# Order of work around three token mixers: preparation of the third moved, taps and tails of the first moved, activation tables fetched earlier

## The chip, the cores and the metric

The kernel runs on one core of one Trainium2 chip. The metric is the device time of one execution, in microseconds. A core has five engines, each with its own instruction stream: TensorE (PE, matrix products and transposes), VectorE (DVE), ScalarE (ACT, activation functions from tables that have to be loaded), GpSimd (POOL) and SyncE (SP, which here only issues DMAs). They wait for each other by semaphores. SBUF is the on-chip memory of 128 partitions, PSUM the one into which PE writes.

## The reference

One inference step of a decoder of two layers, for a prompt of 256 tokens and eight sampled sequences of 4 tokens. All of it is in float32. One layer, cut to what matters:

```python
h = rmsnorm(x, lp['norm_g'])
proj = h @ lp['w_in']
qkv_a, z_a, beta_raw, alpha_raw, f_b, z_b, qkv_c, z_c, gate_raw = jnp.split(proj, offs, axis=-1)
# first mixer: gated delta rule
u_a, dn_buf_new = causal_conv(qkv_a, dn_buf, lp['conv_a'])   # 4 taps; the last 3 rows are an output
q_a, k_a, v_a = jnp.split(jax.nn.silu(u_a), [...], axis=-1)  # q_a, k_a: l2norm by head
o_a, dn_s_new = gated_delta_chunked(q_a, k_a, v_a, g_a, beta, dn_s)   # chunks, triangular systems
o_a = rmsnorm(o_a, lp['onorm_a']) * jax.nn.silu(z_a)
# second mixer: RWKV-7
f_mix = f_b + (prev - f_b) * lp['mu_b']
w_raw = lp['w0_b'] + jnp.tanh(wl_b) @ lp['w2_b'];  a_b = sigmoid(lp['a0_b'] + al_b @ lp['a2_b'])
kk = l2norm(heads(k_b * lp['kk_b']))
y_b, rw_s_new = rwkv7_scan(r_h, logw, k_h, v_h, -kk, kk * a_h, rw_s)
o_b = (groupnorm(y_b) + bonus) * jax.nn.silu(z_b)
# third mixer: block-sparse attention over the paged cache and the new keys
q_c = rope_partial(rmsnorm(heads(q_c), lp['qn_c']), pos)     # the same for k_c
o_c = moba_attention(q_c, pos, k_all, v_all) * jax.nn.silu(z_c)
up = jnp.einsum('blnc,ncd->blnd', jnp.stack([o_a, o_b, o_c], axis=2), lp['w_branch'])
x = x + jnp.sum(sigmoid(gate_raw + lp['b_gate']) * up, axis=2) @ lp['w_out']
x = x + jax.nn.sigmoid(x @ lp['w_pg'] + lp['b_pg']) * (ple @ lp['w_ple'])
```

Outputs are x of both kinds of tokens, the new keys and values, and the new states and last rows of the first two mixers.

## The kernel before

All 288 tokens (256 of the prompt, 32 sampled) go through as the columns of one matrix that lies transposed, 128 channels on the partitions. A projection is 8 matmuls of 128×128 weights by 128×288 for each 128 output channels (`project`, L1092). The weights come through a ring of four SBUF stages; SyncE loads one (L858), 1 MB for two such tiles, when the stage's last projection is done. Three PSUM banks take the projections in turn.

The order of the work is one list of steps, the same for all engines; each engine runs through it and does its part of each step (a method of the step's name in the engine's block). `mixer_steps()` gives the 306 steps of a layer's mixers in order: names with `a_` belong to the first mixer, `b_` to the second, `c_` to the third. `fillers()` gives the projections, cut into "leads" of one K-tile each (one matmul), and their small followers (`z_silu`, `g_tanh`). `schedule()` puts them together: the hand-written list FILL has a number for each mixer step, and so many fillers stand ahead of that step. PE works them off while the other engines prepare the step's operands. The semaphore counts (`S.count`) follow from the list.

The steps that the change and the prediction touch, with their lines:

- First mixer: `a_conv(c)` is the causal convolution of a third of the channels (VectorE L2190 to L2192, part of it on POOL L2735), `a_silu` its activation, `a_sq` the squares. `a_l2(i)` sums them on PE (`sum4`, L1161) and takes the inverse root on ScalarE by Ln and Exp; `a_spread(i)` spreads it by PE (`spread4`, L1168). `a_convout` copies the last three rows ("tails", VectorE L2172), transposes them on PE, evicts them on ScalarE and stores them by POOL (L2713). `a_scale(t)` and `a_pairs(t)` build the chunk matrices, `tri`, `lev_y` and `lev` the inverses of the triangles (PE L1253, L1269, L1275). `a_u(u)` are corrections, u = 2 the sampled sequences' (L1305). `a_sout(0..3)` are their new states: VectorE L2374 masks, PE L1340 multiplies, VectorE L2378 adds, POOL scales the next start (L2770) and stores.
- Second mixer: `b_hist`, `b_shiftout` and `b_mix` prepare the token shift (VectorE L2398 to L2403; POOL clears two buffers, L2790). `b_lora(i)` are the small products behind tanh and sigmoid (PE L1364), `b_kk` and `b_spread` an l2norm, then chunk matrices, triangles and states as in the first mixer, in two groups. `b_fin`, `b_sout`, `b_sdec` end the states, `b_norm1` to `b_norm6` the group norm.
- Third mixer: `c_rms(i)` has 4 of the 8 tiles of queries and keys for each i. ScalarE squares them, PE sums (L1161), ScalarE takes the inverse root; SyncE copies the eight-row halves of each head crosswise (L958), VectorE makes the rotation in three instructions (L2611 to L2613). `c_rope(i)` spreads the roots (L1168) and multiplies (L2619). `c_fetch_k`, `c_fetch_v` fetch pages of the cache (L966). `c_nat` transposes keys and values (PE L1019, ScalarE) and stores them; POOL clears CQX (L2813) and copies the sampled queries into it. `c_keys(g,j)` transposes the past keys; scores, softmax and products follow.

ScalarE has two tables in use, one with Tanh and one with Ln; both have Exp. `logs()` (L1677) loads the second one ahead of an instruction if the other is in place; before Tanh the compiler's own load comes (shown at L1685).

Of the kernel before, what the change touches and what calls it, by code (L numbers as in the profile page):

```python
# [23 lines left out]
US = CONV_W - 1 + LS  # L24
# [77 lines left out]
for _name, _k in PROWS:  # L102
# [95 lines left out]
    "c_turned": {"c_rms": (1, None)},  # L198
# [14 lines left out]
    "c_sw0": {"c_rms": (96, lambda st: st[2] == 0)},  # L213
    "c_sw1": {"c_rms": (96, lambda st: st[2] == 1)},
# [16 lines left out]
    "projected": {"p_a": (1, None), "p_z": (1, None), "p_ba": (1, None), "p_f": (1, None), "p_c": (1, None), "p_g": (1, None), "p_up": (1, None), "p_y": (1, None), "p_pg": (1, None), "p_ple": (1, None)},  # L231
    "square_sums": {"norm": (1, None), "a_l2": (1, None), "b_kk": (1, None), "b_bonus": (1, None), "c_rms": (1, None),
                "a_spread": (1, None), "b_spread": (1, None), "c_rope": (1, None)},
    "squares": {"x_in": (2, None), "p_ple": (2, lambda st: st[1] + 1 < DEPTH), "a_sq": (1, None), "b_kk": (1, None), "c_rms": (1, None)},
# [27 lines left out]
    "c_qx": {"c_nat": (1, lambda st: st[2] == 0)},  # L262
# [3 lines left out]
PROJECTIONS = ("p_a", "p_z", "p_ba", "p_f", "p_c", "p_g", "p_up", "p_y", "p_pg", "p_ple")  # L266
# [33 lines left out]
def mixer_steps():  # L300
# [77 lines left out]
    for g in range(2):  # L378
# [34 lines left out]
        add("b_norm6", g, 1)  # L413
        add("b_s0", g, 0)
# [56 lines left out]
def fillers():  # L471
# [44 lines left out]
    for m in range(4, 8):  # L516
# [6 lines left out]
FILL = [0, 0, 32, 6, 0, 10, 17, 0, 19, 0, 4, 0, 6, 3, 6, 3, 18, 2, 14, 3, 0, 1, 14, 3, 0, 0, 0, 0, 0, 1, 1, 0, 0, 0,  # L523
# [90 lines left out]
def program(nc, A, O):  # L614
# [6 lines left out]
    with ctx:  # L621
# [33 lines left out]
        CT = TRI[:, 896:896 + NA * 27]  # L655
# [52 lines left out]
        BAR1, BN1, BVN1, BRB1, BKK1, BY1 = part(512), part(2, 2, 128), part(2, 128), part(4, 128), part(1024), part(2, 128)  # L708
# [130 lines left out]
        turned = [(h + to, h + of, n) for h in (0, 64) for to, of, n in ((0, 8, 8), (8, 0, 8), (16, 16, 48))]  # L839

# [4 lines left out]
        def _(sp):  # L845
# [107 lines left out]
            def c_rms(l, i):  # L953
                evicted(sp, "p_c", l, 4 * i + 3)
                sp.wait_ge(S.sem("b_done"), S.count("b_done"))
                sp.wait_ge(S.sem("b_snew"), S.count("b_snew"))
                for to, of, n in turned:
                    sp.dma_start(CSW[to:to + n, i, :, :], QC[of:of + n, 4 * i:4 * i + 4, :]).then_inc(S.sem(f"c_sw{i}"), 16)  # L958
# [20 lines left out]
            def c_fetch_v(l, s):  # L979
                if s >= 4:  # L980
# [10 lines left out]
            def y_out(l, m):  # L991
# [8 lines left out]
                if m == 7:  # L1000
                    for name in ("kv_stored", "states_stored", "tail_rows_stored", "y_stored"):
# [3 lines left out]
                      c_rms=c_rms, c_fetch_k=c_fetch_k, c_fetch_v=c_fetch_v, p_up=p_up, y_out=y_out)  # L1005
# [9 lines left out]
        def _(pe):  # L1015
# [646 lines left out]
        def _(act):  # L1662
# [48 lines left out]
            def norm(l):  # L1711
                act.wait_ge(S.sem("param_done"), S.count("param_done"))
# [106 lines left out]
            def a_l2(l, i):  # L1819
                act.wait_ge(S.sem("square_sums"), S.count("square_sums"))  # L1820
# [55 lines left out]
            def a_norm4(l, t):  # L1876
                w = wid(t)
# [12 lines left out]
            def b_lora(l, i):  # L1890
# [966 lines left out]
```

## Time and profile before

| | us |
|---|---|
| median of three runs | 1285.93 |
| the three runs | 1288.49, 1282.99, 1285.93 |
| the profiled execution | 1283.79 |
| its span | 1281.9 |
| PE busy | 1234.9 (96%) |
| VectorE busy | 599.8 (47%) |
| ScalarE busy | 355.2 (28%) |
| POOL busy | 134.7 (11%) |

The profile is of one execution. Its span runs from the first to the last instruction that the profiler has; the execution's own time is 1.9 us longer. "Busy" leaves out semaphore, branch and DMA-issuing instructions. The mean granted clock of PE was 0.989 of full speed. An idle time in brackets, as in `[0.54 <-ACT arena L1685]`, is that of the engine ahead of the instruction, and what ended it: here ScalarE's instruction of line 1685. `<-issue` says that nothing the profile shows ended it.

### The profile page before, as it was taken

How to read it: one execution, taken by the hardware profiler on the slowest of the kernel's cores; microseconds unless marked ns; L12 is line 12 of the kernel's file. 1: busy time of each engine (PE TensorE's matmuls, PEld its weight loads, DVE VectorE, ACT ScalarE, POOL GpSimd, SP SyncE). 2: the span in 40 equal slices, each digit the busy share in tenths (PEclk: the TensorE clock that was granted, in tenths of full speed). 3: DMA queues.
4: the chain of work that ended last, by engine and by line, in shares of the span. 5: the costliest groups of instructions: out<-in, count | busy, mean ns of one | idle time of the engine just before them, and what ended most of it. 6: DMA issues, size and time to landing. Idle time of an engine off the chain costs nothing.

```text
span 1281.9 us, 23685 instructions
## 1 busy us (share of the span) xinstructions
PE 1234.9 (96%) x9382; PEld 920.9 (72%) x9382; DVE 599.8 (47%) x1281; ACT 355.2 (28%) x802; POOL 134.7 (11%) x204
## 2 busy tenths in 40 slices
PE   7998998999999999999999999999999999999998
PEld 5777866787677676767766777567876876776776
DVE  3665456654655533321245654566446455151212
ACT  2333212322233243400224233133223232433001
POOL 0212013020120110000001120320201101100000
PEclk9999999999999999999989999999999999999999
DMA  7732134412301585354236322534123026752621
GB/s 229 224 104 67 44 102 156 121 33 79 93 28 62 160 261 168 117 166 162 67 114 182 106 66 58 158 117 116 35 66 102 19 83 177 252 173 67 213 99 37
DMA packets 143368, 150.15 MB, mean 117 GB/s; under 512 B 15736, under 2 KB 130462, under 8 KB 143132
## 3 DMA queue, kind: packets, MB, share of 16 engines
q1 hardware_dynamic: 139644, 138.75, 35.8%
q0 software_dynamic: 3616, 9.89, 2.7%
q8 instruction: 76, 1.25, 0.4%
q14 instruction: 32, 0.26, 0.1%
HBM read 135.19 MB, written 11.07 MB: 114 GB/s over the span
## 4 chain that ended last, share of the span: by engine, by line
PE 86%; issue 4%; DVE 4%; ACT 2%; SPq 1%; DMA 1%; POOL 1%; ACTq 0%; DVEq 0%; POOLq 0%
PE psum L1092 57%; PE psum L1019 5%; PE psum L1253 3%; PE psum L1269 2%; PE psum L1391 1%; ACT arena L1685 1%; PE psum L1275 1%; PE psum L1134 1%; DVE arena L2192 1%; PE psum L1628 1%; PE psum L1446 1%; PE psum L1230 1%; PE psum L1458 1%; PE psum L1473 1%; PE psum L1577 1%
## 5 line engine op out<-in xcount | busy, mean ns | idle before, releaser
L1092 PE MATMUL psum<-x_b,ring 128*128 128x288 f32 x1296 | 343.1, 414 | 1.9 <-DMA ring<-in_w_in 1.1
L1092 PE MATMUL psum<-x_a,ring 128*128 128x288 f32 x1296 | 343.6, 415 | 0.5 <-DVE x_a L2145 0.4
L1092 PEld LDWEIGHTS psum<-x_b,ring 128*128 128x128 f32 x1296 | 239.9, 192 | 78.5 <-issue 17.2
L1092 PEld LDWEIGHTS psum<-x_a,ring 128*128 128x128 f32 x1296 | 240.4, 192 | 77.7 <-issue 17.0
L1685 ACT ACTIVATE arena<-psum 128x512 f32<-128x512 f32 (+9 forms) x206 | 96.9, 489 | 221.9 <-PE psum L1019 88.8
L1092 PE MATMUL psum<-z,ring 128*128 128x288 f32 x384 | 102.1, 412 | 0.0
L1092 PEld LDWEIGHTS psum<-z,ring 128*128 128x128 f32 x384 | 70.1, 190 | 20.9 <-issue 3.4
L1019 PE MATMUL psum<-consts,arena 128*128 128x128 f32 (+2 forms) x446 | 63.9, 278 | 7.6 <-DMA arena<-in_x_prompt 5.0
L1019 PEld LDWEIGHTS psum<-consts,arena 128*128 128x128 f32 (+2 forms) x446 | 50.7, 143 | 26.5 <-issue 9.8
L1092 PE MATMUL psum<-merged,ring 128*128 128x288 f32 x256 | 64.1, 414 | 3.5 <-issue 2.4
L1685 ACT ACTIVATE arena<-arena 128x256 f32<-128x256 f32 (+7 forms) x104 | 44.8, 464 | 65.8 <-DVE arena L2624 28.9
L1092 PEld LDWEIGHTS psum<-merged,ring 128*128 128x128 f32 x256 | 49.4, 194 | 18.2 <-issue 2.9
L2747 POOL TENSOR_TENSOR triangles<-triangles,consts 128x256 f32<-128x256 f32 (+1 forms) x36 | 24.6, 684 | 282.8 <-DVE triangles L2284 246.2
L1685 ACT ACTIVATE tanh_z<-psum,params_half 128x288 f32<-128x288 f32 x16 | 8.0, 501 | 153.5 <-PE psum L1092 153.5
L1685 ACT ACTIVATE triangles<-psum 128x256 f32<-128x256 f32 (+5 forms) x76 | 25.3, 335 | 89.7 <-PE psum L1253 47.8
L2735 POOL TENSOR_TENSOR arena<-conv_in,params 128x128 f32<-128x128 f32 x24 | 10.4, 432 | 289.1 <-ACT conv_in L1685 275.4
L1685 ACT ACTIVATE conv_in<-psum 128x256 f32<-128x256 f32 (+1 forms) x72 | 21.3, 331 | 65.0 <-PE psum L1092 44.2
L2296 DVE TENSOR_TENSOR triangles<-triangles,psum 128x256 f32<-128x256 f32 (+1 forms) x30 | 12.6, 420 | 54.4 <-PE psum L1275 54.4
L2660 DVE COPY arena<-psum 128x256 f32<-128x256 f32 x4 | 1.7, 424 | 76.0 <-PE psum L1611 76.0
L2151 DVE SCALAR_TENSOR_TENSOR tmp<-tanh_z,psum 128x288 f32<-128x288 f32 x16 | 7.3, 454 | 56.2 <-PE psum L1134 56.2
L2192 DVE SCALAR_TENSOR_TENSOR arena<-conv_in,params,arena 128x256 f32<-128x256 f32 x72 | 32.5, 511 | 0.6
L1275 PE MATMUL psum<-triangles 64*64 64x64 f32 (+1 forms) x528 | 26.5, 226 | 2.7 <-issue 2.7
(345 smaller groups left out, 1570.4 us busy)
## 6 DMA issues: line engine op xcount, KB each, us to landing
ring<-in_w_in SPq DMA_DIRECT2D x72, 1024.0 KB, 5.3
ring<-in_w_branch SPq DMA_DIRECT2D x24, 512.0 KB, 3.5
arena<-in_cache_k SPq DMA_DIRECT2D x32, 256.0 KB, 3.3
arena<-in_cache_v SPq DMA_DIRECT2D x32, 256.0 KB, 3.0
ring<-in_w_out SPq DMA_DIRECT2D x8, 1024.0 KB, 7.4
ring<-in_w_pg SPq DMA_DIRECT2D x8, 1024.0 KB, 5.2
arena<-in_state_dn SPq DMA_DIRECT2D x8, 512.0 KB, 7.9
out_dn_sample<-arena POOLq DMA_DIRECT2D x8, 512.0 KB, 4.3
```

The costliest lines, as they stand in the source:

```text
L1019: return pe.transpose(out, in_, ident[0:w, 0:w])
L1092: ins = mm(out[:, 0:NTOK], lhs, rhs(k), **flags)
L1134: ins = mm(bank()[:, 0:NTOK], WPL[:, k, 128 * m:128 * m + 128], PLT[:, k, :], start=k == 0, stop=k == 1)
L1230: ins = mm(v4(y_bank(t), n)[r, h, :], TC[o, h, 0:n], C("eye64")[o, 0:n], start=True, stop=True)
L1253: ins = mm(v4(y_bank(t), n)[across(r, t), h, :], LM[r, h, 0:n], TI[r, h, 0:n], start=True, stop=True)
L1269: ins = mm(z[r, h, :], TC[o, h, 0:n], Y[o, h, 0:n], start=True, stop=True)
L1275: ins = mm(zt[r if k == NLEV - 2 else o, h, :], Y[o, h, 0:n], TC[o, h, 0:n], start=True, stop=True)
L1391: ins = mm(out, bk[r, pr, x, :], BAR_[r, 2 * w * pr:2 * w * pr + 2 * w], start=True, stop=True)
L1446: ins = mm(M[4][0:w, 64 * hd:64 * hd + 64], vx(of_tile(t, BKK, BKK1), 4, w, w)[:, hd, 0, :], of_tile(t, BVN, BVN1)[0:w, pr, 64 * hh:64 * h ...
L1685: return act.activation(out, in_, func, **kw)
L2192: ins = stt(UC[:, m, 0:SEQ], U[:, m, j:j + SEQ], conv_w(j, m), UC[:, m, 0:SEQ], MUL, ADD)
L2747: tt(LM[0:w, :, 0:n], LT[0:w, :, 0:n], bc(C(f"level{k}", w)[:, 0:n], 1, [w, 4, n]), MUL).then_inc(S.sem(name), 1)
```

## The change

The mixer list goes from 306 to 304 steps, and the fillers from 655 to 661 in a layer (`c_sq`, `c_rms`, `c_turn`, twice each, are now fillers).

1. The first preparation of the third mixer is cut in three (`c_sq`, `c_rms`, `c_turn`) and stands among the fillers behind the first branch's projection `p_up(0, 7)`. Its buffers lie where the second mixer's LW, AA, LC and KK were. SyncE makes 4 crosswise copies of 8 partitions × 2304 elements in place of 12, and POOL clears the buffer for them (128 × 2304). The sums go into a projection bank. The first two key fetches stand behind `b_norm6(1,1)`.
2. `a_conv(2)` stands ahead of `a_spread`; `a_convout` stands behind `tri(0,0)` with buffers of its own in the third slot of Z.
3. `logs()` and the new `tanhs()` load the table ahead of the waits of `norm`, `a_silu`, `a_l2`, `a_norm4`, `b_lora`, `b_kk`, `b_norm4` and `c_sq`.
4. FILL is another list.

```diff
 def mixer_steps():
         add("a_l2", i)
+    add("a_conv", 2)
     for i in range(2):
         add("a_spread", i)
-    add("a_conv", 2)
     add("a_silu", 2)
-    add("a_convout")
     for t in range(2):
         add("a_scale", t)
         add("a_pairs", t)
         add("tri", 0, t)
+        if t == 0:
+            add("a_convout")
...
         add("b_norm6", g, 1)
+        if g == 1:
+            add("c_fetch_k", 0)
+            add("c_fetch_k", 1)
...
-    add("c_rms", 0)
-    add("c_rms", 1)
-    for q in range(4):
-        if q < 2:
-            add("c_fetch_k", q)
-        add("c_fetch_v", q)
     add("c_rope", 0)
     add("c_rope", 1)
+    for q in range(4):
+        add("c_fetch_v", q)
 def fillers():
         whole("p_up", 0, m)
+    for part in ("c_sq", "c_rms", "c_turn"):
+        for i in range(2):
+            out.append((part, i))
 # SyncE
+            def c_sq(l, i):
+                if i == 0:
+                    return
+                evicted(sp, "p_c", l, 7)
+                sp.wait_ge(S.sem("c_cleared"), S.count("c_cleared"))
+                for to, of in swapped:
+                    sp.dma_start(CSW[to:to + 8, :, :, :], QC[of:of + 8, 0:8, :].rearrange("p (i a) n -> p i a n", i=2)).then_inc(S.sem("c_swapped"), 16)
 # PE
             def a_convout(l):
                 pe.wait_ge(S.sem("tails"), S.count("tails"))
-                pe.wait_ge(S.sem("a_unit"), S.count("a_unit"))
-                tr(M[1][0:3 * NA, 384:512], CT[:, 0:3 * NA])
+                pe.wait_ge(S.sem("a_scaled"), S.count("a_scaled"))
+                tr(M[1][0:3 * NA, 384:512], ACT_TAILS[:, 0:3 * NA])
...
             def c_rms(l, i):
-                pe.wait_ge(S.sem("squares"), S.count("squares"))
-                pe.wait_ge(S.sem("b_snew"), S.count("b_snew"))
-
-                sum4(i, SQ[i], C("sum_head"))
+                n = proj_no[S.at]
+                pe.wait_ge(S.sem("squares"), S.count("squares", pos[("c_sq", l, i)]))
+                pe.wait_ge(S.sem(freed()), S.count(freed(), proj_at[n - 3]))
+                for h in range(4):
+                    ins = mm(bank()[32 * h:32 * h + 32, 0:NTOK], C("sum_head"), SQ[:, i, h, :], start=True, stop=True)
+                ins.then_inc(S.sem("projected"), 1)
 # ScalarE
+            def tanhs():
+                if table[0] != "exp_and_others":
+                    table[0] = "exp_and_others"
+                    act.preload_act_table_set(table[0])
...
             def a_l2(l, i):
+                logs()
                 act.wait_ge(S.sem("square_sums"), S.count("square_sums"))
...
+            def c_sq(l, i):
+                logs()
+                evicted(act, "p_c", l, 4 * i + 3)
+                act.wait_ge(S.sem("b_scaled"), S.count("b_scaled", pos[("b_scale", l, 1, 2)]))
+                fn(SQ[:, i, :, :], QC[:, 4 * i:4 * i + 4, :], ACT.Square).then_inc(S.sem("squares"), 1)
 # VectorE
-            def c_rms(l, i):
-                dve.wait_ge(S.sem(f"c_sw{i}"), S.count(f"c_sw{i}"))
+            def c_turn(l, i):
+                dve.wait_ge(S.sem("c_swapped"), S.count("c_swapped"))
                 dve.wait_ge(S.sem("squares"), S.count("squares"))
 # POOL
+            def c_sq(l, i):
+                if i == 0:
+                    pool.wait_ge(S.sem("b_scaled"), S.count("b_scaled", pos[("b_scale", l, 1, 2)]))
+                    pool.memset(CSW[:, :, :, :], 0.0).then_inc(S.sem("c_cleared"), 1)
...
+            def c_fetch_k(l, s):
+                if s == 0:
+                    pool.wait_ge(S.sem("b_done"), S.count("b_done"))
+                    link(pool.memset(CQX[:, :, :, :], 0.0))
```

Fillers ahead of some steps, as the two lists give them (a range counts all from behind the first step to the second):

| steps | before | after |
|---|---|---|
| behind a_conv(1), to a_l2(0) | 23 | 33 |
| all to a_scale(0) | 126 | 116 |
| behind a_s0, to a_u(2) | 11 | 13 |
| a_sout(0), then to (1), (2), (3) | 0, 1, 10, 0 | 0, 0, 15, 0 |
| behind b_hist, to b_lora(0) | 34 | 38 |
| b_kk, b_spread | 17, 8 | 15, 4 |
| behind b_sdec(1,0), to b_norm5(1,2) | 7 | 35 (c_rms and c_turn among them) |
| c_rope(0) with what stood from c_rms on, c_rope(1) | 28, 7 | 9, 3 |
| c_keys(0,0), (0,2), (1,2) | 4, 21, 4 | 3, 14, 11 |

## Rows read from the trace of the kernel before

**Rows 1.** The page: busy us (share of the span), and the chain by engine.
```profile
PE 1234.9 (96%) x9382; PEld 920.9 (72%) x9382; DVE 599.8 (47%) x1281; ACT 355.2 (28%) x802; POOL 134.7 (11%) x204
...
PE 86%; issue 4%; DVE 4%; ACT 2%; SPq 1%; DMA 1%; POOL 1%; ACTq 0%; DVEq 0%; POOLq 0%
```

**Rows 2.** Waits of PE: line, releaser: total us, times, longest us.
```profile
PE psum L1019 <- DMA arena<-in_x_prompt: 5.0, 1, 5.0
PE psum L1364 <- issue: 4.2, 2, 2.1
PE psum L1340 <- DVE arena L2374: 3.6, 2, 1.8
PE psum L1275 <- issue: 3.5, 4, 1.9
PE psum L1092 <- issue: 3.2, 2, 2.4
...
PE psum L1305 <- issue: 1.5, 2, 0.7
...
PE psum L1161 <- ACT arena L1685: 1.3, 2, 0.8
...
PE psum L1168 <- ACT arena L1685: 0.3, 2, 0.2
```

**Rows 3.** Timeline at a_l2: start, us, engine, line, operation, [idle before].
```profile
62.11 1.64 ACT L1685 ACTIVATE arena<-arena 128x1152 f32<-128x1152 f32 x2 [0.54 <-DVE arena L2200]
...
63.33 0.69 PE L1161 MATMUL psum<-arena,consts 128*32 128x288 f32 x8 [0.54 <-ACT arena L1685]
63.77 1.28 ACT L1677 ACT_TABLE_LOAD   x1
```

**Rows 4.** Timeline, one stretch of leads alone.
```profile
86.39 7.06 PE L1092 MATMUL psum<-x_b,ring 128*128 128x288 f32 x28
```

**Rows 5.** Timeline of the four a_sout steps.
```profile
183.97 1.13 PE L1340 MATMUL psum<-arena 32*128 32x512 f32 x4
...
191.70 2.98 DVE L2374 TENSOR_TENSOR arena<-arena,consts 64x512 f32<-64x512 f32 x1
...
192.20 1.92 POOL L2770 TENSOR_TENSOR arena<-arena 128x1024 f32<-128x1024 f32 x1
...
194.74 1.13 PE L1340 MATMUL psum<-arena 32*128 32x512 f32 x4 [1.80 <-DVE arena L2374]
```

**Rows 6.** L2374 alone: ns min/median/max, first and last start.
```profile
L2374 DVE TENSOR_TENSOR arena<-arena,consts x8: 678/684/2984, 182.2 to 824.6; 64x512 f32<-64x512 f32 x8
```

**Rows 7.** Timeline of b_mix and b_lora(0).
```profile
216.09 1.81 POOL L2790 MEMSET arena<- 128x2048 f32 x1
...
216.75 1.23 DVE L2398 TENSOR_TENSOR tmp<-shift_in 128x1024 f32<-128x1024 f32 x1
...
221.37 0.45 ACT L1685 ACTIVATE shift_in<-shift_in 64x288 f32<-64x288 f32 x1 [4.44 <-DVE shift_in L2403]
...
221.91 1.24 PE L1364 MATMUL psum<-shift_in,triangles 64*128 64x288 f32 x8 [2.09 <-issue]
```

**Rows 8.** Line L2398 alone, columns as in rows 6.
```profile
L2398 DVE TENSOR_TENSOR tmp<-shift_in x8: 424/1224/1226, 208.6 to 854.1; 128x1024 f32<-128x1024 f32 x6, 128x256 f32<-128x256 f32 x2
```

**Rows 9.** Timeline from b_fin to the turn of the third mixer.
```profile
427.10 0.38 PE L1019 MATMUL psum<-consts,arena 128*128 128x128 f32 x2
...
428.52 2.17 POOL L2713 DMA_DIRECT2D out_rwkv_prompt<-arena  x4 [24.61 <-ACT arena L1685]
...
444.81 8.77 SPq L958 DMA_DIRECT2D arena<-conv_in  x12
...
452.25 1.42 DVE L2611 SCALAR_TENSOR_TENSOR arena<-arena,turned_gains,consts 128x1152 f32<-128x1152 f32 x1 [7.54 <-DMA arena<-conv_in]
```

**Rows 10.** Timeline of c_rope and c_nat.
```profile
463.62 1.35 DVE L2619 TENSOR_TENSOR conv_in<-conv_in,psum 128x1152 f32<-128x1152 f32 x1 [1.61 <-PE psum L1168]
...
469.94 1.54 ACT L1685 ACTIVATE arena<-psum 128x512 f32<-128x512 f32 x3 [1.21 <-PE psum L1019]
```

More of the change, by code:

```diff
@@ L197 @@
     "c_max": {"c_score": (1, None), "c_sprob": (1, None)},
-    "c_turned": {"c_rms": (1, None)},
+    "c_turned": {"c_turn": (1, None)},
     "c_o": {"c_pv": (1, None)},
@@ L212 @@
     "c_ssc": {"c_past": (1, None)},
-    "c_sw0": {"c_rms": (96, lambda st: st[2] == 0)},
-    "c_sw1": {"c_rms": (96, lambda st: st[2] == 1)},
+    "c_cleared": {"c_sq": (1, lambda st: st[2] == 0)},
+    "c_swapped": {"c_sq": (64, lambda st: st[2] == 1)},
     "corrected": {"a_u": (1, None), "b_u": (1, None)},
@@ L230 @@
     "past_k_ts": {"c_keys": (1, None)},
-    "projected": {"p_a": (1, None), "p_z": (1, None), "p_ba": (1, None), "p_f": (1, None), "p_c": (1, None), "p_g": (1, None), "p_up": (1, None), "p_y": (1, None), "p_pg": (1, None), "p_ple": (1, None)},
-    "square_sums": {"norm": (1, None), "a_l2": (1, None), "b_kk": (1, None), "b_bonus": (1, None), "c_rms": (1, None),
+    "projected": {"p_a": (1, None), "p_z": (1, None), "p_ba": (1, None), "p_f": (1, None), "p_c": (1, None), "p_g": (1, None), "p_up": (1, None), "p_y": (1, None), "p_pg": (1, None), "p_ple": (1, None), "c_rms": (1, None)},
+    "square_sums": {"norm": (1, None), "a_l2": (1, None), "b_kk": (1, None), "b_bonus": (1, None),
                 "a_spread": (1, None), "b_spread": (1, None), "c_rope": (1, None)},
-    "squares": {"x_in": (2, None), "p_ple": (2, lambda st: st[1] + 1 < DEPTH), "a_sq": (1, None), "b_kk": (1, None), "c_rms": (1, None)},
+    "squares": {"x_in": (2, None), "p_ple": (2, lambda st: st[1] + 1 < DEPTH), "a_sq": (1, None), "b_kk": (1, None), "c_sq": (1, None)},
     "start_read": {"a_s0": (1, None), "b_s0": (1, None)},
@@ L265 @@
 }
-PROJECTIONS = ("p_a", "p_z", "p_ba", "p_f", "p_c", "p_g", "p_up", "p_y", "p_pg", "p_ple")
+PROJECTIONS = ("p_a", "p_z", "p_ba", "p_f", "p_c", "p_g", "p_up", "p_y", "p_pg", "p_ple", "c_rms")
 class Steps:
@@ L979, in c_fetch_v @@
             def c_fetch_v(l, s):
+                if s == 0:
+                    sp.wait_ge(S.sem("b_snew"), S.count("b_snew"))
+                    sp.wait_ge(S.sem("states_stored"), S.count("states_stored"))
                 if s >= 4:
@@ L1004, in _ @@
             do = dict(x_in=x_in, params_load=params_load, a_conv=a_conv, b_hist=b_hist, b_scale=b_scale,
-                      c_rms=c_rms, c_fetch_k=c_fetch_k, c_fetch_v=c_fetch_v, p_up=p_up, y_out=y_out)
+                      c_sq=c_sq, c_fetch_k=c_fetch_k, c_fetch_v=c_fetch_v, p_up=p_up, y_out=y_out)
             for i, st in enumerate(order):
@@ L1890, in b_lora @@
             def b_lora(l, i):
+                tanhs()
                 if i == 0:
@@ L2057, in _ @@
                       b_exp=b_exp, b_pairs=b_pairs, b_nat=b_nat, b_st=b_st, b_u=b_u, b_fin=b_fin, b_norm2=b_norm2, b_norm4=b_norm4,
-                      c_rms=c_rms, c_nat=c_nat, c_prob=c_prob, c_keys=c_keys, c_sprob=c_sprob, c_spv=c_spv)
+                      c_sq=c_sq, c_rms=c_rms, c_nat=c_nat, c_prob=c_prob, c_keys=c_keys, c_sprob=c_sprob, c_spv=c_spv)
             for i, st in enumerate(order):
@@ L2166, in a_hist, with tails @@
                 dve.wait_ge(S.sem("hist_in"), S.count("hist_in"))
-            def tails(prompt, sampled, n, *last):
+            def tails(dst, prompt, sampled, n, *last):
                 evicted(dve, *last)
                 k = n * prompt.shape[2]
-                cp(CT[:, 0:k].rearrange("p (c m) -> p m c", m=n), prompt)
-                return cp(CT[:, k:k * (1 + NSEQ)].rearrange("p (s c m) -> p m s c", m=n, s=NSEQ), sampled)
+                cp(dst[:, 0:k].rearrange("p (c m) -> p m c", m=n), prompt)
+                return cp(dst[:, k:k * (1 + NSEQ)].rearrange("p (s c m) -> p m s c", m=n, s=NSEQ), sampled)
             def a_convout(l):
@@ L2690, in _ @@
                       b_scale=b_scale, b_pairs=b_pairs, b_keys=b_keys, b_s0=b_s0, b_w=b_w, b_y=b_y, b_norm1=b_norm1, b_norm3=b_norm3, b_norm5=b_norm5, b_norm6=b_norm6, b_sout=b_sout, b_sdec=b_sdec,
-                      c_rms=c_rms, c_rope=c_rope, c_score=c_score, c_prob=c_prob, c_pv=c_pv, c_out=c_out, c_sprob=c_sprob, c_sout=c_sout,
+                      c_turn=c_turn, c_rope=c_rope, c_score=c_score, c_prob=c_prob, c_pv=c_pv, c_out=c_out, c_sprob=c_sprob, c_sout=c_sout,
                       y_out=y_out)
@@ L2826, in _ @@
             do = dict(a_convout=a_convout, a_conv=a_conv, tri=tri, lev_y=lev_y, a_o=a_o, a_sout=a_sout, b_shiftout=b_shiftout,
-                      b_mix=b_mix, b_fin=b_fin, b_sdec=b_sdec, c_nat=c_nat)
+                      b_mix=b_mix, b_fin=b_fin, b_sdec=b_sdec, c_sq=c_sq, c_fetch_k=c_fetch_k, c_rope=c_rope, c_nat=c_nat)
             for i, st in enumerate(order):
```

85 lines of the change are left out of this document (45 added, 40 removed), and 16 rows, old and new, of the table FILL.

## The prediction, made before the changed kernel had run

> **What bounds the kernel now.** I read four views in this order. First the page: busy shares and the chain that ended last. TensorE (PE) is busy 1234.9 of 1281.9 us, and 86% of the chain lies on it [rows 1]. VectorE, the next, is at 47%. So PE bounds the kernel, and at most 1281.9 − 1234.9 = 47.0 us can be won while PE's instructions stay the same. They do: the matmuls of before are all there after, only in another order (the new `c_rms` has the same eight sums over SQ, in a projection bank). I price PE's busy time at no change.
>
> Then PE's waits, because only those can change the time [rows 2]. Single gaps of 0.3 to 5 us make up about 42 us. "issue" as releaser says that the profile names none; I gave each of these to the step whose instruction follows and looked for the operand that came last. Third, the timeline around each gap. Fourth, the list of steps, with the count of fillers that FILL puts ahead of each, before and after. That gives for each gap the time at which PE arrives and the time at which its operand is there.
>
> The price of a filler comes from the stretch with nothing but fillers: 28 matmuls, 14 leads, in 7.06 us, so 0.504 us a lead [rows 4].
>
> **The change part by part.** All sums are for one layer, then doubled; the layers have the same list.
>
> *a_l2 and the table loads.* PE's sums over the squares of half 1 start 0.54 us late behind ScalarE's Square, and behind them ScalarE loads a table, 1.28 us [rows 3]. After, the list puts 33 leads between a_conv(1) and a_l2(0) instead of 23. PE comes 10 × 0.504 = 5 us later, the squares and the load lie beside that. The gap goes: 0.54 us in layer 0, 0.75 in layer 1, 1.3 together [rows 2]. a_spread's gap (0.3 together) goes as well: 8 leads (4.0 us) stand behind a_l2 before a_spread(0), and the chain to be covered is two Ln–Exp pairs of about 1.05 us with the load already done [rows 3]. Lower bound of this item: 0, if the squares themselves come 5 us later, which needs a later a_conv, whose place ahead is the same in both lists (65 fillers). I take 1.6. The other preloads sit in chains that leads already cover; I cost them at 0, upper bound 1.28 us for each one that ended a PE wait, and rows 2 show no other wait of PE behind such a load.
>
> *a_conv(2) ahead of a_spread, tails behind tri(0,0).* This moves VectorE's convolution of the value taps ahead of two small scalings, and the tail copies (two copies, two transposes' evictions, two POOL stores) beside the triangular system. PE reaches a_scale(0) after 116 leads instead of 126, so it does ask earlier, but the level phase starts after 160 instead of 161. VectorE's work of this stretch was covered by 14 leads of 7.06 us [rows 4] with about 0.9 us over, by my count along the list. I take 0. Bounds: +0.9 a layer if the cover falls short by the two tail copies and their evictions (about 1.3 us together); −0.7 if a small wait inside goes.
>
> *a_u(2).* PE waits 0.73 us a layer for the sampled sequences' first correction [rows 2]. After there are 13 leads since a_s0 instead of 11, 1.0 us more than needed: −1.45 in all.
>
> *a_sout(3).* Before, the four a_sout steps follow each other with 0, 1, 10 and 0 leads ahead. PE starts the first at T0 = 183.97, and the fourth's operand comes at 191.70 + 2.98 = T0 + 10.71; PE stands 1.80 us [rows 5]. After, the counts are 0, 0, 15, 0: PE arrives at T0 + 3 × 1.06 + 15 × 0.504 = T0 + 10.7. The wait shrinks to about 0.1: −1.7 a layer, −3.4 in all. This holds also if VectorE's instruction keeps its 2.98 us, against 0.68 in most of its eight executions [rows 5, 6].
>
> *b_lora(0).* PE stands 2.09 us until the sigmoid's input is ready (221.37 + 0.45; PE starts at 221.91) [rows 7]. Between b_hist and b_lora(0) there are now 38 fillers instead of 34, four more leads, 2.0 us; counted from a_sout(3), whose start VectorE sets in both kernels, 53 instead of 46. VectorE's chain (the rest of the first mixer, then b_mix) is the same instructions. So −2.0 a layer, −4.0 in all. Bound: 0 if that chain is itself released later, by its last projection tile, which is filler 235 in both lists; I keep 4.0.
>
> Behind b_lora: b_kk 17 → 15 leads and b_spread 8 → 4 give up 6 leads. b_kk's 15 leads (7.6 us) meet squares that I find ready 1 us earlier; b_spread's four leads stand where the load of 1.28 us [rows 3] used to be part of the chain. I take 0, upper bound +1 a layer.
>
> *Third mixer under the second.* `c_sq`, `c_rms`, `c_turn` now come as fillers ahead of b_norm5(1,2), with 31 leads among them. PE's part moves, it isn't more. SP issues 4 swap DMAs instead of 12, POOL gets one memset more. `c_turn` sits on VectorE, in order, ahead of b_norm5(1,2), and PE's transposes of b_norm5 wait for that. When? PE's b_fin at 427.10, POOL's four stores at 428.52 + 2.17 = 430.69 [rows 9]. The memset of 2304 elements: 1.81 × 2304/2048 = 2.04 [rows 7], 432.7. SP: one issue is 8.77/12 = 0.73, four are 2.9, 435.7. Landing: the first half's six copies were issued by 444.81 + 4.39 and VectorE starts at 452.25, 3.05 later [rows 9]; 438.7. Six VectorE instructions at most 1.42 each [rows 9]: 8.5, 447.2; b_norm5 itself 0.4: 447.6. PE's arrival: 427.10 + about 8 leads (4.0) + b_sout and b_sdec (2.5) + c_rms (1.2) + 31 leads (15.6) = 450.4. Slack 2.8 us: cost 0. SP's place: behind `c_sq`'s wait for the memset stand ring loads for p_g; the wait and the four issues end by 435.7, about 5 us behind the time at which the next stage comes free, and the other three of the four ring stages hold 16 leads each, 24 us of work: 0. If that cover were gone, a load late by 5 us would cost 5.
>
> Behind it, in the new list c_rope(0) has 9 leads and c_rope(1) 3 where it had 7. VectorE takes 1.35 for c_rope(0) after its wait [rows 10], against 1.5 us of leads plus PE's own part: 0.2 a layer. c_keys(0,0) has 3 leads instead of 4 against ScalarE's three copies that end at 469.94 + 1.54 [rows 10]: 0.3. Together +1.0 for both layers. Bounds: 0 to 3.
>
> *What stays.* x_in's 5.0, w_out's ring load in layer 0 (2.4 of L1092's issue gaps), the gaps in the triangular phases [rows 2]. The largest of the last ones are instruction supply: PE stands with everything ready. New code positions can move them, ±2 us, mean 0.
>
> Sum: −1.6 − 1.45 − 3.4 − 4.0 + 1.0 = −9.4 us. The profiled execution took 1283.79 (span 1281.9), so it becomes 1274.4. The median of three runs is 1285.93, 2.14 above the profiled one: 1276.5.
>
> A rule of the chip speaks against the new memset. The row first: POOL's memset of 1.81 us runs beside VectorE's two-input L2398 at 216.75, which takes 1.23, its usual time [rows 7, 8]. POOL's L2770 reads and writes; beside it L2374 went from 0.68 to 2.98 [rows 5, 6]. The Trainium skill ("SBUF — State Buffer", section "Who interferes with whom") says that a VectorE instruction with two inputs in SBUF contends with a GpSimd instruction that reads SBUF, not with one that only writes. By that rule, the trace agrees, the new memsets cost VectorE nothing.
>
> **The rivals.**
> A, gaps come back: leads are only moved, so a gap filled here opens where they were taken. Behind b_lora 6 leads are gone (3 us a layer), in c_keys(0,2) 7 of 21. If half of the gain is lost: −4.7, 1281.2. For it: the list was taken from b_kk, b_spread and a_scale, and my slacks there are about 1 us. Against: the slacks, as worked out above, are positive at each place.
> B, slower: the swap copies. Four DMAs write 8 partitions each, with twice the bytes per partition of before. If they pass one after another at 3.05 each from the last issue on, 435.7 + 12.2 = 447.9, VectorE ends at 456.8, PE arrives at 450.4 and stands 6.4 us in b_norm5(1,2), 12.8 in all: 1276.5 + 12.8 = 1289.3. It decides from 4.7 us a layer on. For it: few partitions, and nobody before read so large a row. Against: before, 12 copies landed within 3.05 of the issue.
> C, more: the gaps below 0.3 us that the sum leaves out (some 5 us) and part of the supply gaps (L1275 and L1092, 6.7 us [rows 2]) shrink with the steps' new neighbours: −7 more, 1269.5. For it: they belong to steps whose neighbours all change. Against: nothing in the list removes the code that has to be fetched.
> D, no effect of the moves on the ends of the gaps: b_lora and a_sout move with PE, since VectorE's chain starts from PE's steps. −1.6 − 1.45 + 1.0: 1284.
>
> **How the numbers follow.** Forecast 0.5, A 0.15, B 0.12, C 0.13, D 0.07, left for worse than B 0.03. Predicted 1276.5. 0.5% is 6.4 us, about what a measurement of this kernel tells from no change. Faster means below 1279.5: most of the forecast's 0.5, C, and a part of A: 0.63. Slower, above 1292.4: the worse half of B and the rest: 0.10. Same: 0.27. The range goes from C to near B: 1269 to 1287.
>
> **What would show it.** Right: PE's waits list L1364 under 0.5, L1340 under 0.5, L1305 and L1161 near 0, with L1275 and x_in's 5.0 as before; PE busy 1235 ± 2. `c_turn` on VectorE before 448 less the gain so far, with its DMAs landed about 3 us behind the last issue. Wrong: a new PE wait for VectorE in b_norm5(1,2) (B), or new waits at L1161 in b_kk, at L1168 in b_spread or c_rope, or at L1198 in a_scale, above 1 us each (A); or L1364 still at 2 us a layer (D).

## The result, and the profile after

The changed kernel takes 1265.43 us in the median of six runs (1261.98 to 1273.04), the kernel before, run beside it, 1284.46. The ratio is 0.9865, 95% interval 0.9835 to 0.9896: 17.3 us less (13.4 to 21.2) by the ratio, 19.0 by the medians. I had forecast 9.4 less. The direction was right and the size was not: the measured gain is 1.8 times the forecast, and the time lies below the range of 1269 to 1287.

The page of the changed kernel (answering to [rows 1]), one profiled execution:

```profile
span 1268.6 us, 23657 instructions
PE 1235.3 (97%) x9382; PEld 927.5 (73%) x9382; DVE 599.6 (47%) x1281; ACT 354.5 (28%) x802; POOL 139.6 (11%) x206
...
PE 89%; DVE 5%; issue 3%; ACT 1%; POOL 1%; DMA 0%; SPq 0%; ACTq 0%; DVEq 0%; POOLq 0%
```

Span less PE busy is PE's idle time: 33.3 us where it was 47.0. The waits of PE after (answering to [rows 2]):

```profile
PE psum L1031 <- DMA arena<-in_x_prompt: 4.9, 1, 4.9
PE psum L1104 <- DVE merged L2174: 3.0, 2, 1.9
PE psum L1265 <- issue: 2.4, 3, 1.3
...
PE psum L1031 <- ACT arena L1706: 1.0, 2, 0.5
...
PE psum L1180 <- DVE arena L2240: 0.6, 2, 0.3
...
PE psum L1352 <- DVE arena L2409: 0.5, 2, 0.3
...
PE psum L1287 <- issue: 0.4, 1, 0.4
...
PE psum L1376 <- issue: 0.2, 1, 0.2
```

b_lora's 4.2 us (L1376 now) are down to two gaps of 0.14 and 0.15, of which the list shows one; a_sout(3), now L1352, went from 3.6 to 0.5; a_u(2) and a_l2 are gone; L1180 (a_spread(1), 0.28 a layer) and c_keys(0,0) (0.39 a layer) are new. These are the forecast's places. Here are a_sout and b_lora in the timeline (answering to [rows 5, 7]):

```profile
190.19 2.98 DVE L2409 TENSOR_TENSOR arena<-arena,consts 64x512 f32<-64x512 f32 x1
...
193.23 1.13 PE L1352 MATMUL psum<-arena 32*128 32x512 f32 x4 [0.25 <-DVE arena L2409]
...
219.67 0.45 ACT L1706 ACTIVATE shift_in<-shift_in 64x288 f32<-64x288 f32 x1 [0.56 <-DVE shift_in L2438]
...
220.22 1.24 PE L1376 MATMUL psum<-shift_in,triangles 64*128 64x288 f32 x8
```

VectorE's 2.98 us is still there, and PE now comes 0.25 us ahead of its end. But the sum of idle time can't be the whole gain. The same kernel profiled a second time (the run e2 below) had a span of 1260.0 with 35.6 us idle: 8.6 us shorter with 2.3 more idle. So PE's busy time, which I had taken as fixed, isn't. The granted clock shows the larger part of why. These are stretches of the kernel before; the columns are the stretch, its us, busy time of the five engines, then PE's granted clock, DMA share and GB/s:

```profile
119.00:127.00 8.00, 7.57 (x251) 6.94 (x248) 4.00 (x11) 1.54 (x4) 2.92 (x4) 0.79 0.02 4
194.00:202.00 8.00, 7.26 (x23) 4.93 (x24) 3.71 (x4) 0.41 (x1) 3.90 (x4) 0.79 0.64 211
222.00:230.00 8.00, 8.00 (x32) 5.39 (x33) 2.63 (x6) 3.42 (x8) 0.00 (x0) 0.79 0.44 132
570.00:578.00 8.00, 6.30 (x20) 4.79 (x21) 0.76 (x2) 0.00 (x0) 0.00 (x0) 0.79 1.09 348
645.00:653.00 8.00, 6.37 (x18) 4.63 (x19) 5.19 (x15) 1.96 (x5) 0.00 (x0) 0.59 0.34 118
826.00:834.00 8.00, 6.38 (x13) 3.70 (x14) 4.60 (x4) 0.00 (x0) 4.34 (x4) 0.58 0.77 257
```

In each the clock falls within 2 us of the end of one of the large gaps: 1.93 in the triangles, 1.80 at a_sout(3), 2.09 at b_lora(0), 2.4 at p_y(0), 2.3 at the second layer's norm, 1.80 at a_sout(3) again. In each, part of the time was granted at the lower of the clock's two levels, 1.2 instead of 2.4 GHz; a stretch of 8 us at 0.79 has lost 1.7 us, one at 0.58 has lost 3.4. Over the span the loss is (1 − mean granted clock) × span: 0.011 × 1281.9 = 14.1 us before, 0.009 × 1268.6 = 11.4 after, 0.004 × 1260.0 = 5.0 in the second profile after.

| run | median, ratio to before | idle PE, us | mean clock | lost clock, us | lost clock, mean of all executions |
|---|---|---|---|---|---|
| before | 1284.46 | 47.0 | 0.989 | 14.1 | 14.1 |
| before again (e1) | 1286.29, 1.0004 | 43.4 | 0.988 | 15.4 | 14.2 |
| changed | 1265.43, 0.9865 | 33.3 | 0.991 | 11.4 | 9.7 |
| changed again (e2) | 1265.54, 0.9858 | 35.6 | 0.996 | 5.0 | 7.4 |
| e3 moves alone | 1314.41, 1.0237 | 69.0 | 0.982 | 23.6 | 24.7 |
| e4 all but moves | 1284.14, 0.9983 | 46.8 | 0.986 | 18.0 | 13.1 |
| e5 moves aligned | 1272.48, 0.9878 | 36.6 | 0.990 | 12.7 | 8.9 |
| e6 aligned, no preload | 1269.71, 0.9872 | 38.0 | 0.994 | 7.6 | 6.3 |
| e7 long gaps | 1297.59, 1.0082 | 54.3 | 0.990 | 12.9 | 18.6 |
| e8 short gaps | 1287.40, 1.0000 | 48.8 | 0.991 | 11.6 | 8.2 |
| e9 b_lora's gap back | 1271.69, 0.9889 | 40.7 | 0.989 | 14.0 | 9.1 |
| e10 kept busy | 1264.57, 0.9834 | 33.5 | 0.993 | 8.9 | 3.8 |
| e11 parameters later | 1263.45, 0.9821 | 35.2 | 0.997 | 3.8 | 6.0 |
| e12 together | 1261.42, 0.9805 | 32.2 | 0.994 | 7.6 | 2.9 |

Idle time, mean clock and lost clock are of the one profiled execution; the last column has the same loss from the clock and span of every execution of the kernel (4 to 12 of each). For the kernel before it is the mean of the 23 that ran beside e1 to e4. Before, the two profiles have 45.2 idle and 14.8 lost in the mean; after, 34.5 and 8.2. That is 10.7 us of idle time and 6.6 of clock. The mean spans differ by 18.8 us, so 1.5 is left that neither holds. By all executions the clock's part is 14.1 to 14.2 before against 9.7 and 7.4 after, 5.5 us.

A third thing moves between executions, and the mean clock leaves it out: its first record comes 8.1 us into the span in the first profile before, 21.8 in e1, 23.1 in the first profile after, 14.0 in e2. Ahead of it PE runs at the lower clock. Here are the same 16 matmuls, first in the kernel before, at full clock, then in the changed one, whose first record comes in the midst of them:

```profile
16.73 4.15 PE L1092 MATMUL psum<-x_b,ring 128*128 128x288 f32 x16 [1.07 <-DMA ring<-in_w_in]
```

```profile
19.59 5.85 PE L1104 MATMUL psum<-x_b,ring 128*128 128x288 f32 x16
```

PE comes to the same place behind them at 22.86 before and 26.85 in e1, 27.43 after and 24.26 in e2. So between the first two profiles the start alone set the changed kernel back by 4.6 us, and not by its code: in e2 the same code is 3.2 us earlier. In the mean of two profiles it is 1.0.

### The profile page after: what moved, and what is told of

Read it like the earlier page. It is cut to its first block, busy times and chain, and to the rows that moved or that the text cites. A ratio compares the mean times of both kernels' runs of the same rounds, so it can differ in the third digit from the quotient of the medians.

```text
span 1268.6 us, 23657 instructions
## 1 busy us (share of the span) xinstructions
PE 1235.3 (97%) x9382; PEld 927.5 (73%) x9382; DVE 599.6 (47%) x1281; ACT 354.5 (28%) x802; POOL 139.6 (11%) x206
## 3 DMA queue, kind: packets, MB, share of 16 engines
q8 instruction: 76, 1.25, 0.4%
## 4 chain that ended last, share of the span: by engine, by line
PE 89%; DVE 5%; issue 3%; ACT 1%; POOL 1%; DMA 0%; SPq 0%; ACTq 0%; DVEq 0%; POOLq 0%
PE psum L1104 59%; PE psum L1031 5%; PE psum L1265 3%; PE psum L1281 2%; PE psum L1403 1%; PE psum L1287 1%; PE psum L1146 1%; ACT arena L1706 1%; PE psum L1643 1%; DVE arena L2227 1%; PE psum L1470 1%; PE psum L1485 1%; PE psum L1458 1%; PE psum L1242 1%; PE psum L1495 1%
## 5 line engine op out<-in xcount | busy, mean ns | idle before, releaser
L1706 ACT ACTIVATE triangles<-psum 128x256 f32<-128x256 f32 (+4 forms) x72 | 23.9, 332 | 88.0 <-PE psum L1265 44.9
L2770 POOL TENSOR_TENSOR arena<-conv_in,params 128x128 f32<-128x128 f32 x24 | 10.7, 447 | 284.6 <-ACT conv_in L1706 271.2
L1706 ACT ACTIVATE shift_in<-psum 128x256 f32<-128x256 f32 (+1 forms) x52 | 12.3, 288 | 54.8 <-PE psum L1104 54.6
```

Source lines behind the costliest of these rows:

```text
L1706: return act.activation(out, in_, func, **kw)
```

## The experiments

**e1 and e2: both kernels again.**

> The kernel before, unchanged, timed against itself. Theory 'spread': the ratio is 1 within about 0.4%, and its profile shows the gaps with a named operand (b_lora(0) 2 x 2.1, a_sout(3) 2 x 1.8, a_u(2) 2 x 0.7) within 0.1 us of the first profile, while the gaps without one in the triangular phases (3.5 and 3.0 us at two lines) differ by 1 to 3 us from execution to execution. Rival 'fixed': the gaps without an operand come back in the same places with the same lengths, since they are the code's own; then the 3.7 us by which they are shorter after the change belong to the change.

> The changed kernel, unchanged. Theory 'spread': its ratio to before is about 0.990 (the 13.3 us between the two profiled executions, or less), and the 0.9865 of the first comparison was in part the spread of the runs. Rival 'fixed': 0.9865 again, and a gain of 4 us that single profiled executions don't show.

Measured 1.0004 (0.9982 to 1.0026) and 0.9858 (0.9822 to 0.9894). The rival held for e1: the gaps without a named operand came back in the same places, 0.2 to 0.3 us off in length (1.72 where it was 1.93, 0.97 for 0.70, 0.95 for 1.22, 0.76 for 1.04), so they are the code's. The gain is 17 to 18 us by the ratios, 19 to 21 by the medians, and the first profile of the changed kernel was the second longest of its six executions. What differs most between two executions of one kernel is the clock: 0.991 and 0.996 after.

**e3: the moves of fillers alone.**

```diff
 # before's FILL, with the changed kernel's numbers from lev_y(0,0,1) to b_bonus; tables loaded ahead of waits
-        0, 0, 0, 3, 8, 5, 5, 0, 1, 7, 3, 0, 0, 12, 0, 0, 15, 0, 19, 5, 17, 8, 12, 5, ...
+        1, 0, 0, 0, 2, 11, 2, 4, 0, 0, 4, 11, 0, 0, 12, 2, 1, 15, 3, 20, 5, 15, 4, 13, 5, ...
```

> Before, with the changed kernel's counts of fillers from the first level of the first mixer to b_spread, and with the tables loaded ahead of waits; no move of the third mixer, of a_conv(2) or of the tails. Theory 'moves': PE's gaps at a_u(2), a_sout(3) and b_lora(0) are gone, -8.4 us, a_l2 stays (its load was never the wait): 0.9934 of before. Rival 'preparation': the fillers were free only because the third mixer was prepared earlier, and new gaps of 5 us or more open at b_kk, b_spread or behind.

Measured 1.0237 (1.0204 to 1.0271), 28 us slower by the medians. Neither theory gave that. The list of PE's waits in e3:

```profile
PE psum L1019 <- DMA turned_gains<-params: 13.2, 2, 6.6
PE psum L1364 <- issue: 10.1, 2, 5.0
PE psum L1161 <- ACT tmp L1691: 6.1, 2, 3.0
```

a_u(2) and a_sout(3) were cured as in the changed kernel, but 6.6 us a layer opened at b_hist, and b_lora(0) and b_kk, whose chains start there, followed. The timeline of SyncE in e3, and then in e5, says why:

```profile
205.47 0.37 SPq L858 DMA_DIRECT2D ring<-in_w_in  x1
205.94 0.50 SPq L929 DMA_DIRECT2D triangles<-in_state_rwkv_shift  x1
206.48 4.03 SPq L934 DMA_DIRECT2D turned_gains<-params  x6
210.56 0.59 SPq L937 DMA_DIRECT2D triangles<-in_w_b  x1
211.19 0.59 SPq L937 DMA_DIRECT2D triangles<-in_a_b  x1
```

```profile
195.84 0.98 SPq L937 DMA_DIRECT2D triangles<-in_w_b  x1
196.86 0.59 SPq L937 DMA_DIRECT2D triangles<-in_a_b  x1
201.48 8.24 SPq L858 DMA_DIRECT2D ring<-in_w_in  x2
```

SyncE issues a ring load as soon as the list has passed the last projection of the stage, and waits for that projection first. In e3 that projection, p_z(1,1), stood one filler ahead of b_hist. The ring load (205.47) therefore stood ahead of b_hist's nine small loads, and these could be issued only when PE had got there.

**e5 and e6: the moves, one filler later.**

```diff
-  a_pairs(1): 14 fillers, b_exp(0,0): 5
+  a_pairs(1): 13 fillers, b_exp(0,0): 6
```

> As the run with the moves alone, but one filler less ahead of a_pairs(1) and one more behind b_bonus, so that every filler from the first level to b_bonus stands where it stands in the changed kernel (there each stood one place early, p_z(1,1) ended ahead of b_hist instead of behind it, and SyncE's ring load stood ahead of b_hist's parameter loads). Theory 'one filler': the gaps of 6.6 at b_hist, 5.0 at b_lora(0) and 3.0 at b_kk are gone with it; PE's gaps at a_u(2), a_sout(3), b_lora(0) are gone too, 8.4 us, and with them four stretches at the lower clock, which cost 1.7 to 3.4 each, 7 us; 0.988 of before. Rival 'preparation': the moves need the third mixer's earlier preparation or the other changes; 1.00 or slower again.

> The same without the tables loaded ahead of waits. Theory 'preloads carry it': b_kk and b_spread have 6 fillers less, and the load of 1.28 us in their chains shows again: gaps of about 1 us a layer at b_spread or b_kk, 0.990 to 0.993 of before. Rival 'preloads are nothing': within 0.1% of the run with them.

Measured 0.9878 (0.9851 to 0.9906) with the preloads and 0.9872 (0.9850 to 0.9893) without. 'One filler' is shown: the same list, moved by one place, is worth 1.0237 − 0.9878, 46 us. And the moves by themselves bring 14 to 17 us, where the whole change brings 17 to 21. PE's waits in e5:

```profile
PE psum L1019 <- DMA arena<-in_x_prompt: 5.1, 1, 5.1
PE psum L1253 <- issue: 3.9, 4, 1.6
PE psum L1092 <- DVE merged L2152: 3.1, 2, 2.0
...
PE psum L1161 <- ACT arena L1691: 1.3, 2, 0.7
...
PE psum L1340 <- DVE arena L2387: 0.5, 2, 0.3
```

L1364 and L1305 are no longer in it, L1340 is down to the changed kernel's 0.5, and a_l2's 1.3 is left. No stretch of lower clock stands behind a_sout(3) or b_lora(0), in e5 or in e6. Without the preloads one gap of 0.39 a layer stood at b_spread, and the time was the same within intervals of 3 to 4 us: the preloads are worth nothing that these runs can measure.

**e4: everything but the moves.**

```diff
 # changed kernel's FILL, with before's numbers from lev_y(0,0,1) to b_bonus
```

> Changed kernel, with the counts of before from the first level of the first mixer to b_spread. Theory 'moves': the gaps at a_u(2), a_sout(3) and b_lora(0) are back (8.4 us), and what is left of the gain is about 1.3 at a_l2, less 1 behind c_rope, with whatever the supply gaps do: 0.996 to 1.000 of before. Rival 'preparation': 0.991 or less, the three titled parts carry half of the gain or more.

Measured 0.9983 (0.9959 to 1.0008). Its waits have a_sout(3) and b_lora(0) back, and a new one of 1.1 a layer at b_kk (L1173):

```profile
PE psum L1376 <- issue: 4.6, 2, 2.3
PE psum L1352 <- DVE arena L2409: 3.6, 2, 1.8
...
PE psum L1173 <- ACT tmp L1706: 2.2, 2, 1.1
```

The clock came back with the gaps: it fell again behind both a_sout(3), at 197 and 825 us, and behind both b_lora(0), at 224 and 856, 8.5 us of loss in all; over its twelve executions the loss is 13.1 in the mean, as before the change. The third mixer prepared early, the taps and tails moved and the tables fetched ahead are together worth between −1 and 5 us, 2 by the middle value; the new gaps at b_kk are in that.

**e7 and e8: the clock by itself.**

```diff
 # PE, behind the chosen steps
+                if i in paused:
+                    pe.wait_ge(S.sem("c_cleared"), S.count("c_cleared"))
 # POOL (e7: four clears of 128 x 500 behind p_g 15, 17, 19, 21; e8: one of 128 x 256 behind 16 projections a layer)
+                if i in paused:
+                    pool.wait_ge(S.sem("projected"), S.count("projected"))
+                    pool.memset(SCRATCH[:, :], 0.0).then_inc(S.sem("c_cleared"), 1)
```

> Changed kernel, in which PE waits behind four p_g projections of each layer (15, 17, 19, 21) for four small clears on POOL, about 2.3 us each time: 8 gaps, 18 us of idle time added. Theory 'clock': behind each such gap PE's granted clock falls to the lower level for a stretch, as behind the gaps of 1.8 to 2.3 us before the change, and costs 1.7 to 3.4 us more each: 32 to 45 us in all, 1.012 to 1.022 of before. Rival 'gaps only': 18 us or less, 1.001 of before, PE busy as in the changed kernel.

> Changed kernel, in which PE waits behind sixteen projections of each layer (p_g 16 to 23, p_up(1,*)) for one small clear on POOL, about 0.5 us each time: 32 gaps, 16 us of idle time added. Theory 'clock': short gaps leave the clock alone, only the idle time itself is lost, 16 us or less: 0.998 of before. Rival 'any idle time lowers the clock': as with the long gaps, 30 us or more, 1.01 of before or slower.

e7 had eight gaps of 2.35 to 2.41 us, 19.1 in all, and came out at 1.0082 (1.0056 to 1.0108), 32 us above e2 by the medians. That is 13 more than the idle time, 1.6 a gap. The granted clock of its five executions says the same by another way: 18.6 us lost in the mean where the changed kernel lost 7.4 and 9.7, 9 to 11 us more, 1.1 to 1.4 a gap. In its profile, the shortest of its runs, four of the eight gaps were followed by a lower clock:

```profile
467.66 6.56 PE L1106 MATMUL psum<-x_b,ring 128*128 128x288 f32 x19 [2.35 <-POOL scratch L2884]
```

```profile
469.00:473.00 4.00, 4.00 (x11) 2.89 (x10) 0.00 (x0) 1.02 (x1) 0.00 (x0) 0.57 0.62 197
483.00:487.00 4.00, 4.00 (x60) 2.68 (x53) 0.99 (x4) 0.00 (x0) 0.00 (x0) 0.60 0.22 82
503.00:507.00 4.00, 4.00 (x14) 2.97 (x13) 0.43 (x1) 0.29 (x2) 0.00 (x0) 0.57 0.62 212
1114.00:1118.00 4.00, 3.70 (x30) 1.72 (x34) 0.00 (x0) 0.00 (x0) 0.25 (x1) 0.57 0.72 228
```

e8 had 32 gaps of 0.43 to 0.49, 15.4 in all, and came out at 1.0000 (0.9981 to 1.0018), 22 above e2. None of these gaps was followed by a lower clock in its profile, and its ten executions lost 8.2 us of clock in the mean, no more than the changed kernel. The 6.5 us beyond the idle time are left: PE busy less lost clock is 1231 there against 1219 to 1226 in the other runs (1227 in e10, which does 4 us more work), which would be 0.2 us or so for each stop that the gap's record doesn't hold. I call that likely, not shown. So 'clock' holds: 19.1 us of idle time in long gaps cost 32 us, 9 to 11 of them clock; 15.4 us in short ones cost 22, none of them clock.

**e9: b_lora's four fillers given back.**

```diff
-  b_lora(0): 20 fillers, b_kk: 15, b_spread: 4
+  b_lora(0): 16 fillers, b_kk: 17, b_spread: 6
```

> Changed kernel, with the four fillers that it had gained ahead of b_lora(0) put behind it (two ahead of b_kk, two ahead of b_spread). Theory 'gap and clock': PE waits 2.0 us in each layer again, and behind one or both gaps the lower clock costs 1.7 to 3.4: 5.5 to 9 us slower than the changed kernel, 0.9905 to 0.993 of before. Rival 'gap only': 4.0 us, 0.989.

Measured 0.9889 (0.9865 to 0.9913), 6.2 us above e2 by the medians and 4.0 by the ratios. The gap of 2.09 is back in both layers, with 0.60 at b_kk; one of the two was followed by a lower clock (847 to 851 at 0.57). The intervals are as wide as the difference between the theories, and the lost clock of its six executions, 9.1 us, lies between the changed kernel's 7.4 and 9.7: inconclusive between them.

**e10: PE kept busy in the norm's wait.**

```diff
                 else:
+                    for k in range(8):
+                        mm(M[4][:, 0:NTOK], C("ones"), MG[:, k, :], start=k == 0, stop=k == 7)
                     pe.wait_ge(S.sem("squares"), S.count("squares"))
```

> Changed kernel, with eight matmuls whose result nobody reads ahead of PE's wait in the second layer's norm (a gap of 2.13 us, behind which the clock was low in every profile). Theory 'clock': the wait ends at the same time, the gap shrinks to 0.1, and the 16 matmuls of the first projections take 4.0 us instead of 6.7: 2.5 to 3.4 us faster than the changed kernel, 0.983 to 0.984 of before. Rival 'clock falls by itself there': no change, or slower by what the added matmuls push back.

Measured 0.9834 (0.9810 to 0.9857), 1 to 3 us better than e2. First the second profile of the changed kernel, then e10, the second layer's norm on PE:

```profile
634.16 0.75 PE L1071 MATMUL psum<-tmp,consts 128*128 128x288 f32 x2 [2.13 <-DVE tmp L2192]
...
636.78 6.71 PE L1104 MATMUL psum<-x_a,ring 128*128 128x288 f32 x16 [0.24 <-DVE x_a L2140]
```

```profile
642.28 4.04 PE L1071 MATMUL psum<-merged,consts 128*128 128x288 f32 x16
646.16 0.65 PE L1073 MATMUL psum<-tmp,consts 128*128 128x288 f32 x2
...
648.68 3.63 PE L1106 MATMUL psum<-x_a,ring 128*128 128x288 f32 x14 [0.94 <-DVE x_a L2142]
```

The clock stayed up: 14 matmuls in 3.63, against 16 in 6.71 behind the gap, 2.6 us. The table's 8.9 us for e10 is of its longest execution; the six lost 3.8 in the mean, 3.6 to 5.9 less than the changed kernel. But one product is two instructions in float32, so eight products took 4.04 us where the gap was 2.13, and pushed the norm back by 1.8. Four would have fitted; that wasn't run.

**e11 and e12: the parameter loads, and all of it together.**

```diff
-        if l + 1 < DEPTH:
-            order.append(("params_load", l + 1))
         for m in range(8):
             add("p_up", 2, m)
+        if l + 1 < DEPTH:
+            order.append(("params_load", l + 1))
```

> Changed kernel, with params_load of the second layer's parameters behind the p_up(2,*) projections instead of ahead of them. Theory 'SyncE's queue': the load of w_out for p_y(0) stands behind 22 small parameter loads; with these behind it PE's 1.9 to 2.4 us in p_y(0) of layer 0 shrinks to the 1.1 of layer 1: 1 us, and now and then 1.7 of clock, 0.984 to 0.985. Rival 'the parameters come late instead': a new wait in params_t, the same or slower.

> Changed kernel with both of these, one filler from c_rope(0) to b_norm5(1,2), and one from c_keys(0,2) to c_keys(0,0). Sum of the parts: 3 at norm, 1 to 2.5 at p_y(0), 1.0 at b_norm5 and 0.8 at c_keys: 6 to 7 us faster than the changed kernel, 0.980 to 0.981 of before.

e11: 0.9821 (0.9792 to 0.9851). p_y(0) waits 1.09 in both layers now, where it had 1.9 (2.2 in e2) and 1.1; the parameters weren't missed. e12: 0.9805 (0.9778 to 0.9832), the fastest of all, 1261.42. That is 4 to 7 us better than the changed kernel and 25 better than before.

```profile
PE psum L1031 <- DMA arena<-in_x_prompt: 5.1, 1, 5.1
PE psum L1267 <- issue: 3.0, 4, 1.6
PE psum L1106 <- DVE merged L2176: 2.2, 2, 1.1
```

The intervals of e11 and e12 touch that of e2; that each part gives what was expected isn't shown, that the whole beats before is.

## Why the prediction was wrong

The step that failed is its first: "I price PE's busy time at no change." I read the mean clock of 0.989 as a constant. It is the sum of a few stretches at half clock, nearly all behind gaps of 1.6 us and more, and three of these gaps (a_sout(3) in both layers, b_lora(0) in the first) were among those that I forecast away. Behind them the clock lost 1.7 + 3.4 + 1.7 = 6.8 us, in the profile that I had and again in e1; behind the second layer's b_lora(0) it lost nothing in either. The missing term measures 6.6 us in the mean of the profiles, 5.5 by all executions. With it the forecast would have been 15 to 16.

The step's own sign, "PE busy 1235 ± 2", was met in the first profile of the changed kernel, 1235.3, and that was chance. The 6.8 us were gone from it, but the late rise of the clock at the start (4.6 us) and a stretch of 10 us at half clock (last section) stood in their place; e2 has 1224.4, and e1 1240.8 for the kernel before.

The idle time, step by step, first profiles of both. The items add up to −8.1 of the −9.4 that I forecast; the profiles' idle time fell by 13.8, and the other 5.7 are in the supply gaps and in places that the sum left out.

- a_l2: forecast −1.3, measured −1.29. a_spread −0.3, measured −0.32 at i = 0, +0.56 at i = 1, where PE now waits for VectorE's L2240 and not for the table.
- a_u(2): −1.45, measured −1.45.
- a_sout(3): −3.4, measured −3.09; left over were 0.25 a layer, I had said 0.1.
- b_lora(0): −4.0, measured −3.88.
- c_rope and c_keys(0,0): +1.0, measured +0.78, all of it in c_keys(0,0).
- The swap copies: by the first profile of the changed kernel they were issued by 433.15 and landed by 437.87, 4.72 behind the last issue instead of 3.05 (5.4 in the second layer, 5.3 in e2). The first issue came 0.8 behind the memset's end, since two ring loads held SyncE until 429.89. The two took 2.5 of my 2.8 us of slack:

```profile
427.23 2.04 POOL L2845 MEMSET arena<- 128x2304 f32 x1
...
430.08 3.07 SPq L969 DMA_DIRECT2D arena<-conv_in  x4
...
437.87 1.42 DVE L2646 SCALAR_TENSOR_TENSOR arena<-arena,turned_gains,consts 128x1152 f32<-128x1152 f32 x1 [4.97 <-issue]
```

  b_norm5(1,2) waited 0 and 0.63 us in the first profile, 0.67 and 1.11 in the second. So rival B's place was right, at 0.6 to 1.8 of its 12.8 us; its mechanism, four landings one after another, was not: that would have been 12.2 behind the last issue. The memset's 2.04 us was as forecast. VectorE's instructions beside it (L2624, L2595, L2169 at 0.68, 0.41, 0.45) took their usual time, but none of them has two inputs in SBUF, so what such a one would do beside this memset no run shows.
- The supply gaps in the triangles: forecast 0 ± 2, measured 6.5 and 5.9 before, 3.4 in both profiles after: about −2.8, the largest (1.93) gone. That is a part of what rival C had named. e1 shows that they belong to the code, and so this part to the change. norm_x's gap of 1.19 doesn't: it was absent in e1, and stood at 0.9 to 1.2 us in just the five profiles whose clock was up by 9 us (before, e4, e6, e7, e12).
- A slip of reading that moves nothing in the sum: PE's gaps of 0.3 us and more are 34.3 us together and those below 8.4, where I wrote 42 and 5.

Rival A (gaps come back behind b_lora) was wrong here, and right in e3 by a way that I hadn't thought of: a filler list also orders SyncE's queue. Rival D was wrong: the two gaps it would have kept are gone. My reading that the moves of fillers carry the gain, which stood in the sum but was never said, is what e4 to e6 show.

## What to carry to other kernels

Where PE bounds the time, price a gap by what it does to the granted clock as well: look at the stretches behind the large gaps one by one, since the mean hides them, and fill the largest gaps first. The 14 profiles have 51 gaps of PE of 1.5 to 2.5 us; behind 37 of them the clock fell, and that cost 1.7 or 3.4 us more (once 6.8). Of their 35 gaps of 0.9 to 1.25 us, first 30 and last 40 us left out, none had it. A us of idle time cost 1.7 us in e7's long gaps and 1.4 in e8's short ones. And before a list of fillers is shifted by one, see which DMAs on SyncE's queue stand behind the weight load that the shift moves.

## What the runs showed of the hardware

The clock fell without a large gap too: in the first profile of the changed kernel a stretch of 10 us was granted at half clock with no gap above 0.43 us before it, behind the small products of the second mixer. e5, e8 and e10 have it at the same place; the second profile of the same code doesn't:

```profile
279.00:289.00 10.00, 10.00 (x47) 9.30 (x45) 0.88 (x3) 0.38 (x1) 0.00 (x0) 0.50 0.00 0
```

Such a stretch is 5 us. The start is another source: over the 14 profiles the clock's first record comes between 8.1 and 24.2 us, with no relation to the edits that I can see, and PE passes the same place between 22.7 and 28.5. e2's six executions lie between 1261.21 and 1273.23; their recorded clock loss goes from 5.0 to 11.4, half of that. What decides either is open.
